# Moving the gather and two transposes inside the expert loop, and loading the sigmoid table ahead

## The reference

```
x1  = x + merged @ w_out
h2  = rms_norm(x1, norm2_g)
logits = h2 @ w_router + b_router            # 32 experts
top 4 per token, softmax over the 4 selected -> combine[t, e]
for e in range(32):
    a = clamped_swiglu(h2 @ w_up[e] + b_up[e])        # min, sigmoid(1.702*g), clip, (lin + 1)
    out += combine[:, e] * (a @ w_down[e] + b_down[e])
return x1 + out
```

## Time and profile before

| | |
|---|---|
| median of 3 runs | 1282.13 us (1281.88 to 1283.11) |
| profiled execution: its time | 1281.22 us |
| its span, first to last instruction | 1279.4 us |
| mean granted TensorE clock | 0.955 of full |
| PE busy | 1182.9 us (92%) |
| DVE busy, ACT busy | 380.8 us, 313.6 us |
| moved by DMA | 449.99 MB |

### The profile page before, as it was taken

One profiled execution on the slowest core, in us unless ns is written; L12 is line 12 of the kernel. 1 busy time (PEld: TensorE's weight loads), 2 busy tenths in 40 slices (PEclk: granted clock), 3 DMA queues, 4 the chain that ended last, 5 costly groups with the idle time before them and its releaser, 6 DMA issues.

```text
span 1279.4 us, 13646 instructions
## 1 busy us (share of the span) xinstructions
PE 1182.9 (92%) x5596; PEld 549.9 (43%) x5596; DVE 380.8 (30%) x711; ACT 313.6 (25%) x432; POOL 80.2 (6%) x98
## 2 busy tenths in 40 slices
PE   8999999998999999999999998999999999999997
PEld 7789888863333333333333333333333333333332
DVE  5676855642211111111112122221111211211112
ACT  6655544431111111111111111111111111111111
POOL 6343320000000000000000000000000000000000
PEclk9999999999999999999999999999999999999998
DMA  8545489679999999999999999999999999999900
GB/s 298 166 139 178 145 302 381 226 309 376 411 411 410 411 410 413 410 411 411 410 410 407 416 408 407 411 417 401 411 413 412 405 404 407 410 412 409 412 37 33
DMA packets 51466, 449.99 MB, mean 352 GB/s; under 512 B 4610, under 2 KB 4738, under 8 KB 26836
## 3 DMA queue, kind: packets, MB, share of 16 engines
q1 hardware_dynamic: 49936, 447.76, 86.3%
q10 hardware_dynamic: 1476, 1.42, 0.4%
HBM read 448.12 MB, written 1.05 MB: 351 GB/s over the span
## 4 chain that ended last, share of the span: by engine, by line
PE 80%; DVE 10%; ACT 8%; issue 2%; POOL 1%; DMA 0%; DVEq 0%; ACTq 0%; SPq 0%; POOLq 0%
PE aux L1561 31%; PE aux L1631 22%; PE acc L1413 11%; PE aux L1494 5%; ACT L820 3%; PE acc L1406 3%; PE aux L1613 2%; DVE sig L1189 2%; DVE glu L1180 2%; DVE sig L1183 2%; PE aux L1506 2%; ACT sig L820 2%; DVE aux L1185 2%; ACT aT L822 2%; PE aux L1581 1%
## 5 line engine op out<-in xcount | busy, mean ns | idle before, releaser
L1561 PE MATMUL aux<-ring,xgT 128*64 128x512 f32 x2048 | 463.5, 594 | 0.8 <-DVE xgT L1129 0.8
L1631 PE MATMUL aux<-ring,aT 128*64 128x512 f32 x1024 | 288.0, 714 | 11.2 <-ACT aT L822 11.2
L1561 PEld LDWEIGHTS aux<-ring,xgT 128*64 128x64 f32 x2048 | 143.7, 137 | 264.3 <-issue 253.8
L1631 PEld LDWEIGHTS aux<-ring,aT 128*64 128x64 f32 x1024 | 80.0, 160 | 177.7 <-issue 157.0
L1180 DVE TENSOR_SCALAR glu<-aux 128x512 f32<-128x512 f32 x32 | 22.1, 691 | 418.9 <-PE aux L1561 418.9
L852 DVE TENSOR_TENSOR w_lo<-raw,w_hi 128x1024 fp32r<-128x1024 f32 x80 | 104.2, 1322 | 50.4 <-ACT w_hi L643 50.3
L643 ACT ACTIVATE w_hi<-raw 128x1024 fp32r<-128x1024 f32 x80 | 84.1, 1059 | 88.5 <-PE acc L1413 73.0
L825 ACT ACTIVATE y_hi<-aux,slot_w 128x512 fp32r<-128x512 f32 x32 | 22.0, 687 | 302.7 <-PE aux L1631 302.7
L820 ACT ACT_TABLE_LOAD x32 | 41.1, 1283 | 198.5 <-DVE glu L1180 198.5
L1613 PE MATMUL aux<-ident,sig 128*128 128x128 f32 x128 | 24.0, 310 | 70.0 <-DVE sig L1189 70.0
L1413 PE MATMUL acc<-w_hi,hT_hi 128*128 128x512 f32 x188 | 75.7, 403 | 1.4 <-DVE hT_lo L864 1.3
(11 more groups left out here) (281 smaller groups left out, 1053.3 us busy)
## 6 DMA issues: line engine op xcount, KB each, us to landing
ring<-w_up_dram SPq DMA_DIRECT2D x128, 2048.0 KB, 12.3
ring<-w_down_dram SPq DMA_DIRECT2D x64, 2048.0 KB, 9.1
raw<-w_in_dram SPq DMA_DIRECT2D x25, 1024.0 KB, 5.2
raw<-w_branch_dram SPq DMA_DIRECT2D x6, 1024.0 KB, 5.2
raw<-w_kv_dram SPq DMA_DIRECT2D x4, 1024.0 KB, 5.2
raw<-w_out_dram SPq DMA_DIRECT2D x4, 1024.0 KB, 5.1
x<-x_dram SPq DMA_DIRECT2D x2, 512.0 KB, 4.1
raw<-w_in_dram SPq DMA_DIRECT2D x2, 512.0 KB, 5.9
```

Source lines behind the costliest of these rows:

```text
L1561: ins = nc.tensor.matmul(bank[64 * half:64 * half + 64, :], xgT[:, k], w_rows[:, c0 + half * W:c0 + (half + 1) * W], start=(k == 0), stop= ...
L1631: ins = nc.tensor.matmul(bank_cy[64 * half:64 * half + 64, :], aT[:, j, 64 * ff_half:64 * ff_half + 64], w_rows[:, half * W:(half + 1) * W ...
```

## The change

In PE's item, the gather of the next item stands behind the scatter instead of between the up products, the transposes of the combine weights stand right behind those of the activation (and use `bank_lin`), and the transposes of the gathered tokens stand after m = 1 of the down products (and use `bank_glu`). On ACT, an activation of one column with Sigmoid opens each item, and the copy of the gathered tokens follows the real sigmoid. On DVE the combine weights are built once `gathered` has come, and the gathered tokens are moved after `pickT`. `xg_tok` no longer shares memory with `sig` but with `y_hi`, `pick_w` with `y_lo`. To find room, the tables `ss` and `rstd` are packed. `keep_up` issues 8, 4 and 3 products at three places instead of 4 and 4 at two.

```diff
-WARM_UP, KEEP_UP = 14, 4
+WARM_UP, KEEP_UP = 14, (8, 4, 3)
+STAT = [0, 2, 4, 20, 36, 44, 52, 56]
-        xg_tok = sig
+        xg_tok = sb("xg_tok", [P, W], F32, Region(nc, start_y_hi, start_y_lo))
+        pick_w = sb("pick_w", [P, NT, 2, SLOTS], F32, Region(nc, start_y_lo, end_y_lo))
...
             def item(n):                                    # ACT
-                copy_gathered(n + 1)
-                act.wait_ge(xg_turned, n + 1)
+                nc.scalar.activation(ms[:, 0:1], minus_half[:, 0:1], ACT.Sigmoid)
                 act.wait_ge(glu_ready, n)
                 nc.scalar.activation(sig[:], glu[:], ACT.Sigmoid, scale=ALPHA).then_inc(sig_ready, 1)
+                copy_gathered(n + 1)
                 act.wait_ge(aT_done, n)
...
-                move_gathered(n + 1)                        # DVE, behind a_ready
+                dve.wait_ge(gathered, n + 1)
                 build_pick_w(bass.ds(n - 1, 1))
                 build_pick(bass.ds(n + 1, 1))
                 dve.wait_ge(pick_wT_done, n)
-                ... pickT and slot_w from bank_t
+                ... pickT and slot_w from bank_lin
+                move_gathered(n + 1)
                 dve.wait_ge(y_done, n)
...
-            keep_up()                                       # PE, ahead of the loop
+            keep_up(0)
...
+            keep_up(1)
             gather(1)
-            keep_up()
+            keep_up(2)
+            pe.wait_ge(extra_ready, 1)
             turn_gathered(1)
...
                 pe.wait_ge(xg_ready, n)                     # PE, item
-                if first_item:
-                    pe.wait_ge(extra_ready, 1)
+                if not first_item:
+                    pe.wait_ge(pickT_ready, n - 1)
...
-                    if k == 3:
-                        if not first_item:
-                            pe.wait_ge(y_hi_ready, n - 1)
-                            pe.wait_ge(y_lo_ready, n - 1)
-                        gather(n + 1)
-                    if k == 5:
-                        turn_gathered(n + 1)
...
                     scatter(n - 1, second_item)
+                gather(n + 1)
                 pe.wait_ge(a_ready, n)
                 ... transposes of sig into bank_t
                 ins.then_inc(aT_done, 1)
+                pe.wait_ge(pick_w_ready, n)
+                for t in range(NT):
+                    ins = nc.tensor.transpose(bank_lin[:, t * P:(t + 1) * P],
+                                              pick_w[:, t].rearrange("p a s -> p (a s)"), ident[:])
+                ins.then_inc(pick_wT_done, 1)
-                pe.wait_ge(xg_ready, n + 1)
+                pe.wait_ge(xg_tok_ready, n + 1)
                 ... down bias, then down products m = 0 to 7
-                    if m == 3:
-                        pe.wait_ge(pick_w_ready, n)
-                        ... transposes of pick_w into bank_t
+                    if m == 1:
+                        turn_gathered(n + 1)
```

More of the change, by code:

```diff
@@ L155, in hybrid_block @@
         iota = sb("iota", [P, SLOTS], F32)
-        ss = sb("ss", [P, 7, 16], F32)
+        ss = sb("ss", [P, STAT[7]], F32)
         ms = sb("ms", [P, 16], F32)
-        rstd = sb("rstd", [P, 7, 16], F32)
+        rstd = sb("rstd", [P, STAT[7]], F32)
         minus_half = sb("minus_half", [P, 16], F32)
@@ L166, in hybrid_block @@
         iota_e = sb("iota_e", [32, 2], F32)
+        pick = sb("pick", [P, NT, SLOTS], F32)
         meta = sb("meta", [1, EXTRA_COLS + 1], I32)
@@ L243, in hybrid_block @@
         xgT = sb("xgT", [P, KD, SLOTS], F32, m)
+        start_aT = m.at
         aT = sb("aT", [P, KB, P], F32, m)
-        start_t = m.at
+        start_y_hi = m.at
         y_hi = sb("y_hi", [P, W], F32R, m)
+        start_y_lo = m.at
         y_lo = sb("y_lo", [P, W], F32R, m)
+        end_y_lo = m.at
         m = Region(nc, start_gate, end_gate)
@@ L250, in hybrid_block @@
         sig = sb("sig", [P, W], F32, m)
-        xg_tok = sig
[L253 to L258, removed]
+        xg_tok = sb("xg_tok", [P, W], F32, Region(nc, start_y_hi, start_y_lo))
+        pick_w = sb("pick_w", [P, NT, 2, SLOTS], F32, Region(nc, start_y_lo, end_y_lo))
+        ones_f = sb("ones_f", [32, P], F32, Region(nc, start_gate, end_gate))
+        posT = sb("posT", [32, 2, NT, P], F32, Region(nc, start_aT, start_y_hi))
+        t = Region(nc, start_y_lo, end_y_lo)
         logits = sb("logits", [P, NT, NEXP], F32, t)
@@ L524, in rstd_of @@
                 pool.wait_ge(ss_ready[n], 1)
-                chained(nc.gpsimd.tensor_scalar(ms[:, 0:count], ss[:, n, 0:count], 1.0 / width, eps,
+                chained(nc.gpsimd.tensor_scalar(ms[:, 0:count], ss[:, STAT[n]:STAT[n] + count], 1.0 / width, eps,
                                                 ALU.mult, ALU.add))
-                nc.gpsimd.tensor_tensor(rstd[:, n, 0:count], ms[:, 0:count], minus_half[:, 0:count],
+                nc.gpsimd.tensor_tensor(rstd[:, STAT[n]:STAT[n] + count], ms[:, 0:count], minus_half[:, 0:count],
                                         ALU.pow).then_inc(rstd_ready, 1)
@@ L647, in _ @@
                 act.wait_ge(x_loaded[t], 16)
-                nc.scalar.activation(xs[:, t], x1[:, t], ACT.Square, accum_out=ss[:, 0, t:t + 1]
+                nc.scalar.activation(xs[:, t], x1[:, t], ACT.Square, accum_out=ss[:, STAT[0] + t:STAT[0] + t + 1]
                                      ).then_inc(ss_ready[0], 1)
@@ L774, in _ @@
                         act.wait_ge(mem_loaded[t], 16)
-                        ins = nc.scalar.activation(scratch[t], mem_sb[:, t], ACT.Square, accum_out=ss[:, 1, t:t + 1])
+                        ins = nc.scalar.activation(scratch[t], mem_sb[:, t], ACT.Square, accum_out=ss[:, STAT[1] + t:STAT[1] + t + 1])
                     ins.then_inc(ss_ready[1], 1)
@@ L1066, in _ @@
                     for t in range(NT):
-                        nc.vector.tensor_scalar(xs[:, t], mem_sb[:, t], rstd[:, 1, t:t + 1], None,
+                        nc.vector.tensor_scalar(xs[:, t], mem_sb[:, t], rstd[:, STAT[1] + t:STAT[1] + t + 1], None,
                                                 ALU.mult).then_inc(xs_ready, 1)
@@ L1084, in _ @@
                 ins = nc.vector.scalar_tensor_tensor(logits[:, t], acc[2][:, t * NEXP:(t + 1) * NEXP],
-                                                     rstd[:, 6, t:t + 1], spread[:], ALU.mult, ALU.add)
+                                                     rstd[:, STAT[6] + t:STAT[6] + t + 1], spread[:], ALU.mult, ALU.add)
             chained(ins)
@@ L1196, in item @@
                 dve.wait_ge(pick_wT_done, n)
-                nc.vector.tensor_scalar(pickT[:].rearrange("p t s -> p (t s)"), bank_t[:, 0:NT * P], 0.0, None,
+                nc.vector.tensor_scalar(pickT[:].rearrange("p t s -> p (t s)"), bank_lin[:, 0:NT * P], 0.0, None,
                                         ALU.is_gt)
-                nc.vector.tensor_reduce(slot_w[:], bank_t[:, 0:NT * P], AX, ALU.add).then_inc(pickT_ready, 1)
+                nc.vector.tensor_reduce(slot_w[:], bank_lin[:, 0:NT * P], AX, ALU.add).then_inc(pickT_ready, 1)
+                move_gathered(n + 1)
                 dve.wait_ge(y_done, n)
@@ L1469, in _, with keep_up @@
             pe.wait_ge(const_built, built("tables"))
-            def keep_up():
-                for _ in range(KEEP_UP):
+            def keep_up(stretch):
+                for _ in range(KEEP_UP[stretch]):
                     nc.tensor.matmul(acc[0][:], ones_bf[0:96], bias_up[:, 0:W], start=True, stop=True)
-            keep_up()
+            keep_up(0)
             pe.wait_ge(chosen_ready, 1)
@@ L1505, in turn_gathered @@
                     rows = xg_tok[:, c * n:(c + 1) * n].rearrange("s (p j) -> s j p", j=UP_ROWS)[:, j]
-                    ins = nc.tensor.transpose(bank_cy[:, q * P:(q + 1) * P], rows, ident[:])
+                    ins = nc.tensor.transpose(bank_glu[:, q * P:(q + 1) * P], rows, ident[:])
                 ins.then_inc(xg_turned, 1)
+            keep_up(1)
             gather(1)
-            keep_up()
+            keep_up(2)
+            pe.wait_ge(extra_ready, 1)
             turn_gathered(1)
```

21 lines of the change are left out of this document (10 added, 11 removed).

## The result

| | before | changed |
|---|---|---|
| median | 1282.21 us (1281.88 to 1283.11, 4 runs) | 1200.01 us (1199.87 to 1200.48, 4 runs) |
| profiled execution: time, span | 1281.22, 1279.4 us | 1200.07, 1198.3 us |
| granted clock, mean | 0.955 | 0.996 |

The ratio is 0.9359, with a 95% interval of 0.9342 to 0.9375: 82 us faster. The forecast was 1192 us, with 1182 to 1222 as its range.

The account below looks back on a forecast made before the run. PE's order bounds the kernel; once PE's item falls to 26.1 us, the weights' DMA does. Last byte 1172.5 + 1 + 2.1 + 1.9 + 11.4 = 1189 us span, plus 1.8 and 0.9: 1192 us, range 1182 to 1222.

Parts of the forecast that it names:

- The bound, and that it would change hands: Expert loop: PE's order sets 30.73 us an item; after the change the weights' DMA binds from item 15, near 650 us.
- The part sums: PE's item: 14.3 to the scatter, 4.2 to the down products, 7.6 for these; 26.1 us, 4.6 less than before.
- U: In PE's item, the start of the scatter, from which the prediction times activation, transposes and down products.
- The rate: Ring's weight stream: 381.6 MB from 285 us on at 430 GB/s, last byte at 1172.5 us.
- Behind the last byte: Last item: 1 us semaphore, 2.1 to the down products' first half with turning, 1.9 low clock, 11.4 to span end.
- 1 us for the semaphore: After the ring's last byte: an estimated allowance of 1 us until its landing is signalled.
- the 1.9 us for a spell of low clock: Last item: one low-clock spell of PE, likely where it waits for every chunk, adds 1.9 us.
- The 0.9 us added for the median: From profiled execution to reported time: the median was taken to lie 0.9 us above that execution.
- A: Weight stream: bursts of 430 GB/s don't last, the mean stays at 409; 1237 us, chance 0.12.
- B: Down products: the low clock stays in each item, PE's item is 28.1 to 28.4 us; 1203 us, chance 0.06.
- C: Items from 15 on: PE at the low clock while waiting for weights, slower; 1367 us with f = 0.5, chance 0.04.
- D: Whole loop: no DMA bound, PE's 26.1 us for all 32 items; 1131 us, chance 0.03.

Follow-up runs that it names:

- Experiment 2: The kernel before, with ring loads from the 13th chunk on cut to half their bytes: 1283.6 us, ratio 1.0008.
- experiment 1: The changed kernel, with ring loads from the 13th chunk on cut to half their bytes: 1144.46 us, ratio 0.8925.
- Experiment 10: The changed kernel with 18 of the 48 pairs of up and down products left out in each item, loads whole: 1195.57 us, ratio 0.9326.
- experiment 3: The kernel before with only the one-column Sigmoid added at the head of ACT's item, loads cut to half: 1188.15 us, ratio 0.9265.
- experiment 5: The kernel before with six filler products per item ahead of PE's wait for the activation, loads cut to half: 1229.45 us, ratio 0.9584.
- experiment 4: The kernel before with only the one-column Sigmoid added at the head of ACT's item, loads whole: 1198.72 us, ratio 0.9349.
- experiment 7: The changed kernel without the one-column Sigmoid, loads whole: 1200.06 us, ratio 0.9362.
- experiment 8: The changed kernel with Exp instead of Sigmoid in the one-column activation, loads cut to half: 1144.49 us, ratio 0.8922.
- experiment 9: The changed kernel with Exp instead of Sigmoid in the one-column activation, loads whole: 1200.29 us, ratio 0.9356.

## Why the prediction was right, and where its numbers were off

**The bound, and that it would change hands.** Shown. Experiment 2 takes the memory off the kernel before without effect, and experiment 1 takes it off the changed kernel, which gains 56 us. Experiment 10 takes 7.7 us an item off PE, some 240 us in all, and the time falls by 4.4. From the part sums the two were to meet at item 15, and they did.

**The part sums.** 26.1 us forecast, 26.48 measured. The up part is right (14.31 against 14.27). Between U and the down products 4.2 became 4.51. The scatter takes 1.13 us where the sum had four steps of 0.23, though the earlier trace rows has 0.33 for the first of them, and the gather 1.86 where the sum had 1.72: switches between kinds of product, for which the sum had nothing. The idle 0.2 us in front of pick_w is there (0.17), with the clock at 1.00. Only in the last item does this reach the time, with some 0.3 us.

**The rate.** The first mis-sized term: 430 GB/s from stretches of 18 and 30 us, 427 over 300 us. 381.6 MB take 894 us instead of 887: 6.2 us.

**Behind the last byte.** The second: 16.5 us forecast between the mean end of the bytes and the end of the span, and 1198.3 - 1178.7 = 19.6 measured. This 3.1 us is what is left of three differences, one of which went the other way.

First, the sum divided all bytes by the mean rate and allowed 1 us for the semaphore. The last chunk, issued at 1133.4, lands 50.9 us later, at 1184.3, which is 5.6 us behind the mean end and 4.6 more than allowed:

```profile
L450 SPq DMA_DIRECT2D ring<-w_down_dram x2: 4247/4248/4249, 1129.1 to 1133.4; - x2
...
DMA to landing us min/median/max: 50.3/50.6/50.9
```

The landings of the chunks show where this comes from. They are 4.9 us apart, but for four of them that come 6.2 to 6.4 us behind the one before, at 488.4, 705.6, 937.8 and 1169.7 us, and the later ones never make it up. Four times 1.4 us are the 5.6 us, while the mean rate stays at 427 GB/s.

Second, the 1.9 us for a spell of low clock were not due. The spell came, at 1169.68, and was over by 1173, before c3 of the last item, the last chunk that PE had to wait for, landed at 1174.5 (issued at 1124.8, 49.7 us to landing). PE's last 16 up products, 3.6 us that end at U = 1178.19, start no earlier than that. So the spell lay hidden in front of a landing. Third, PE takes about 0.4 us longer from there to the end than the sum had, 0.3 of them between U and the down products. 4.6 - 1.9 + 0.4 = 3.1.

The two terms make 6.2 + 3.1 = 9.3 us, which is the whole miss of the span (1189 against 1198.3). That it isn't 11 us is luck: a term that was not due covered part of one that was too small. The 0.9 us added for the median were not needed either: the median lies at the profiled execution.

**The rivals.** A (the mean stays at 409) fell with the slices. B (the low clock stays) fell with the changed kernel's 26.48 us an item at a clock of 1.00; experiments 3 and 5 add that the low clock came with 2.15 and 0.35 us of idle time, and not with 0.87 or 0.75 and the same 0.35. B's price was not worked out soundly: 26.1 + 1.85 is 27.95 us an item, not 28.1 to 28.4, and with that the sum gives 1190 us, which the forecast couldn't be told from by the time alone. C (slower, PE at 1.2 GHz while it waits) didn't come: from 700 to 1160 us, with PE waiting for weights, the mean clock is 1.00. In experiment 10, with over four times the waiting, it fell to 0.88, and the rate of the weights stayed at 427 GB/s. A PE with so many waits and nothing to spare wasn't run. D fell at once; 1131 was its sum and experiment 1, which takes the memory away, gives 1144.

**What the prediction didn't ask.** It added the parts up to 4.6 us and cut the sum at the memory. It didn't ask which part alone reaches that floor. The last item's glu starts at 1176.6 us in the changed kernel and at 1176.5 in experiment 4, without the moves; from 303.6 at the first, 31 items of 28.2 us get PE there, an estimate from experiment 4. So the first 2.6 us an item are worth time, and the one line of experiment 4 brings 3. Added to that line the moves are worth nothing, or less: they put the gather and one set of transposes behind the last landing that PE waits for. PE's timeline of the last item in experiment 4:

```profile
1174.47 3.65 PE L1562 MATMUL aux<-ring,xgT 128*64 128x512 f32 x16 [0.30 <-DMA ring<-w_up_dram]
1178.05 0.50 PE L1552 MATMUL acc<-y_hi,pickT 64*128 64x512 f32 x2
...
1185.51 3.65 PE L1632 MATMUL aux<-ring,aT 128*64 128x512 f32 x16
1190.97 0.50 PE L1552 MATMUL acc<-y_hi,pickT 64*128 64x512 f32 x2 [1.80 <-DVE y_lo L1205]
```

And in the changed kernel:

```profile
1169.68 8.58 PE L1569 MATMUL aux<-ring,xgT 128*64 128x512 f32 x32 [2.61 <-DMA ring<-w_up_dram]
1178.19 0.50 PE L1559 MATMUL acc<-y_hi,pickT 64*128 64x512 f32 x2
...
1185.20 5.37 PE L1637 MATMUL aux<-ring,aT 128*64 128x512 f32 x24
1192.37 0.50 PE L1559 MATMUL acc<-y_hi,pickT 64*128 64x512 f32 x2 [1.80 <-DVE y_lo L1210]
```

From U to the last scatter are 12.92 us with the one line and 14.18 with the whole change. This 1.26 us and a U that comes 0.14 us later make the 1.4 us between the two profiled spans (1196.9 and 1198.3). In the times it is 1.3 us: 1198.18 to 1198.79 in experiment 4, 1199.87 to 1200.48 for the changed kernel and 1199.94 to 1200.46 for the moves without the line (experiment 7). That is 0.1%: the ranges of the times don't meet, the intervals of the ratios overlap. So the kernel before with one line more is at least as fast as the whole change.

What isn't shown is the moves with the table load truly in the chain. In the item shown first (from 444.85) DVE's last product ends at 461.07 and PE gets to the transposes at 462.11: 1.04 us of slack against 1.28 us of load, so PE would wait some 0.3 us an item, under the memory's cover. That is argued, from numbers of one item, and wasn't run.

## What to carry to other kernels

When an engine at its own pace lies only a little above a full queue (here 30.7 against 29.4 us), ask of every part how far it must go, not what all of them add up to; the cheapest one may reach the floor. Count an idle gap of PE with the products behind it, which ran at 0.55 of the clock for 3.8 us here. And for a stream that bounds to the end, look at when each chunk lands, not only at the mean rate, and time the work behind the last landing that is waited for: work that is moved late in the item, where it is free in the middle of the loop, stands in the open in the last one.

## What was not expected of the hardware

**A table load can wait in an activation's place.** Told in experiments 8 and 9: with two waits on the sigmoid the 1.28 us load stood behind glu_ready; with one wait it ran 10 us ahead. In that place the load cost 1.28 us of chain, and through the clock 1.69 more (experiment 3).

**The landing of a chunk can slip, and the stream doesn't catch up.** By its DMA's time to landing, c2 of the last item landed at 1169.7, 1.4 us later than the 4.9 us rhythm of the others, and the chunks behind it kept the rhythm from there. It is the last of the four slips told above. From each to the next are eight items. One fetch of instructions by DMA falls into the stretch from 1164 to 1170 us (DMA queues: packets, MB, share of 16 engines):

```profile
q8 instruction: 1, 0.02, 1.1%
```

One falls into each of the stretches that end in the other three slips too (482 to 489, 700 to 706, 932 to 938 us). But such a fetch comes once per item, and with seven of eight no landing slips. If it is the cause, it must also hit the engine that is behind already. This is a guess; no run took the fetches away.
